# Gate and up products of an expert job in one pass of 256 columns, in a two-layer encoder with a mixture of experts

## What is computed

```
...
def expert_block(args):
    xblk, e = args
    return (jax.nn.silu(xblk @ w1[e]) * (xblk @ w3[e])) @ w2[e]
...
x = x + _hier_moe(_rmsnorm(x, ffn_norm_w[l]), ..., expert_w_gate[l], expert_w_up[l], expert_w_down[l])
...
```

## Time and profile before

| | us |
|---|---|
| median of 3 runs | 1587.78 |
| lowest and highest | 1585.37, 1592.27 |
| the profiled execution | 1591.66 |
| its span, first to last instruction | 1589.8 |
| TensorE busy (matmul records) in the span | 1325.3 (83%) |
| VectorE busy | 661.5 (42%) |
| ScalarE busy | 461.5 (29%) |
| HBM read | 488.09 MB, 308 GB/s over the span |

### The profile page before, as it was taken

One profiled execution on the slowest core, in us unless ns is written; L12 is line 12 of the kernel. 1 busy time (PEld: TensorE's weight loads), 2 busy tenths in 40 slices (PEclk: granted clock), 3 DMA queues, 4 the chain that ended last, 5 costly groups with the idle time before them and its releaser, 6 DMA issues. The chain is left out here.

```text
span 1589.8 us, 46384 instructions
## 1 busy us (share of the span) xinstructions
PE 1325.3 (83%) x19436; PEld 1016.1 (64%) x19437; DVE 661.5 (42%) x1618; ACT 461.5 (29%) x952; POOL 120.8 (8%) x108
## 2 busy tenths in 40 slices
PE   7998899998788776678799988999888887776775
PEld 6787687766555554455578876787666655554554
DVE  6666856663222111112186777666622221111112
ACT  3455645542111100001054565554411110100101
POOL 2002530000000000000020045200000000000000
PEclk9998999999999888989999999999999998888888
DMA  9531224589999999999974220445999999999996
GB/s 342 201 128 54 67 93 173 211 356 380 425 424 428 429 427 427 428 428 427 413 270 159 106 83 30 159 166 209 389 414 410 426 428 427 427 429 427 428 428 267
DMA packets 80204, 490.60 MB, mean 309 GB/s; under 512 B 13263, under 2 KB 15847, under 8 KB 52455
## 3 DMA queue, kind: packets, MB, share of 16 engines
q1 hardware_dynamic: 80102, 489.16, 75.8%
HBM read 488.09 MB, written 1.05 MB: 308 GB/s over the span
## 5 line engine op out<-in xcount | busy, mean ns | idle before, releaser
L2067 PE MATMUL ps<-ring,arena 128*32 128x128 f32 x5504 | 204.0, 308 | 119.1 <-DMA ring<-in_expert_w_gate_dram 75.0
L2067 PEld LDWEIGHTS ps<-ring,arena 128*32 128x32 f32 x5504 | 177.0, 124 | 157.7 <-DMA ring<-in_expert_w_gate_dram 77.2
L2149 ACT ACTIVATE arena<-ps 128x128 f32<-128x128 f32 x66 | 18.3, 278 | 479.8 <-PE ps L2067 479.8
L2067 PE MATMUL ps<-arena 128*32 128x128 f32 x2688 | 98.7, 305 | 51.1 <-DMA arena<-in_expert_w_gate_dram 34.6
L2250 DVE COPY arena<-ps 128x256 f32<-128x256 f32 x68 | 28.9, 425 | 249.2 <-PE ps L2033 249.0
L2067 PEld LDWEIGHTS ps<-arena 128*32 128x32 f32 x2688 | 86.1, 124 | 69.9 <-DMA arena<-in_expert_w_gate_dram 39.9
L489 POOL TENSOR_TENSOR small<-small,cst 128x8 f32<-128x8 f32 (+1 forms) x21 | 27.7, 1318 | 1209.6 <-DVE small L763 450.4
L1822 DVE TENSOR_TENSOR w_low<-ring,w_high 128x512 fp32r<-128x512 f32 x126 | 85.7, 705 | 51.8 <-ACT w_high L1746 51.8
L2091 PE MATMUL ps<-ring,arena 128*32 128x256 f32 x1440 | 94.6, 399 | 9.9 <-DMA ring<-in_expert_w_down_dram 6.8
L2311 DVE TENSOR_TENSOR arena<-ps,arena 128x128 f32<-128x128 f32 x66 | 25.0, 380 | 185.1 <-ACT arena L2149 185.1
L1746 ACT ACTIVATE w_high<-ring 128x512 fp32r<-128x512 f32 x126 | 77.2, 635 | 74.3 <-PE ps L1682 62.0
(11 more groups left out here) (374 smaller groups left out, 2474.7 us busy)
## 6 DMA issues: line engine op xcount, KB each, us to landing
ring<-in_expert_w_gate_dram SPq DMA_DIRECT2D x42, 2048.0 KB, 40.3
ring<-in_expert_w_up_dram SPq DMA_DIRECT2D x42, 2048.0 KB, 40.6
ring<-in_w_in_dram SPq DMA_DIRECT2D x28, 2048.0 KB, 7.7
ring<-in_expert_w_down_dram SPq DMA_DIRECT2D x22, 2048.0 KB, 41.2
ring<-in_expert_w_down_dram SPq DMA_DIRECT2D x44, 1024.0 KB, 37.4
arena<-in_expert_w_up_dram SPq DMA_DIRECT2D x20, 2048.0 KB, 41.0
arena<-in_expert_w_gate_dram SPq DMA_DIRECT2D x20, 2048.0 KB, 39.8
arena<-in_expert_w_down_dram SPq DMA_DIRECT2D x20, 2048.0 KB, 41.7
```

The costliest lines, as they stand in the source:

```text
L2067: ins = pe.matmul(bank_b[32 * g:32 * g + 32, u * P:(u + 1) * P], xg[:, c], spare[u][:, c, g] if from_spare else w[:, u, c, g], start=(c == ...
```

## The change

For the very first job of a layer (i = 0, k = 0) all stays as it was. Every other job waits for its gate slot and its up slot, then runs 32 matmuls of 256 columns, each with the gate columns and the up columns of one (c, g) side by side, into the first 256 columns of `bank_b`; then it counts `m_gu` up. The gather of job J + 1 comes behind this pass. SP waits for `m_gu` ahead of both loads of the pair, except for the first job's gate slot, for which it still waits for `m_gate`. For the job of expert 3 to read both spare slots in one view, `tenth` and `eleventh` become the halves of one tensor, `spare_pair`; their places in memory are the same.

```diff
@@ -135,8 +135,10 @@
     x_sb = sb("x_sb", NT * D_MODEL)
     hT = sb("hT", KC * SEQ)
     assert start_of["hT"] == start_of["x_sb"] + 4 * NT * D_MODEL
-    tenth = nc.alloc_sbuf_tensor_at("tenth_slot", [P, 4096], F32, offset=start_of["x_sb"])
-    eleventh = sb("eleventh_slot", 4096)
+    sb("eleventh_slot", 4096)
+    assert start_of["eleventh_slot"] == start_of["x_sb"] + 4 * 4096
+    spare_pair = nc.alloc_sbuf_tensor_at("spare_pair", [P, 2 * 4096], F32, offset=start_of["x_sb"])
+    tenth, eleventh = spare_pair[:, 0:4096], spare_pair[:, 4096:2 * 4096]
     xn = sb("xn", NT * D_MODEL)
     cst = sb("cst", K_ALL)
     arena = sb("arena", 16160)
@@ -1914,7 +1916,7 @@
                 def refill(i, k, load, pair=True):
                     count(i, k)
                     if pair:
-                        sp.wait_ge(m_gate, sp.snap(ended))
+                        sp.wait_ge(m_gate if isinstance(i, int) and (i, k) == (0, 0) else m_gu, sp.snap(ended))
                         load(i, 3 * k)
                         sp.wait_ge(m_gu, sp.snap(ended))
                         load(i, 3 * k + 1)
@@ -2053,22 +2055,28 @@
                     pe.wait_ge(m_xg, J)
                     landing = i * 16 + 16 if isinstance(i, int) else pe.snap(i * 16 + 16)
                     w = gate_up(k)
-                    spare = [t[:, :].rearrange("p (c g f) -> p c g f", c=KC, g=4) for t in (tenth, eleventh)]
-                    for u in range(2):
-                        from_spare = k == 0 and isinstance(i, int) and i == 1
-                        if from_spare:
-                            pe.wait_ge(m_land[3 * SETS + u], (32, 16)[u])
-                        elif k == 0:
-                            pe.wait_ge(m_land[u], max(i * 16, 16) if isinstance(i, int) else pe.snap(i * 16))
+                    if k == 0 and isinstance(i, int) and i == 0:
+                        for u in range(2):
+                            pe.wait_ge(m_land[u], 16)
+                            for c in range(KC):
+                                for g in range(4):
+                                    ins = pe.matmul(bank_b[32 * g:32 * g + 32, u * P:(u + 1) * P], xg[:, c], w[:, u, c, g],
+                                                    start=(c == 0), stop=(c == KC - 1))
+                            ins.then_inc((m_gate, m_gu)[u], 1)
+                    else:
+                        if k == 0 and isinstance(i, int) and i == 1:
+                            w = spare_pair[:, :].rearrange("p (u c g f) -> p u c g f", u=2, c=KC, g=4)
+                            pe.wait_ge(m_land[3 * SETS], 32)
+                            pe.wait_ge(m_land[3 * SETS + 1], 16)
                         else:
-                            pe.wait_ge(m_land[3 * k + u], landing)
+                            for u in range(2):
+                                pe.wait_ge(m_land[3 * k + u], pe.snap(i * 16) if k == 0 else landing)
                         for c in range(KC):
                             for g in range(4):
-                                ins = pe.matmul(bank_b[32 * g:32 * g + 32, u * P:(u + 1) * P], xg[:, c], spare[u][:, c, g] if from_spare else w[:, u, c, g],
+                                ins = pe.matmul(bank_b[32 * g:32 * g + 32, 0:2 * P].rearrange("p (u f) -> p u f", u=2), xg[:, c], w[:, :, c, g],
                                                 start=(c == 0), stop=(c == KC - 1))
-                        ins.then_inc((m_gate, m_gu)[u], 1)
-                        if u == (1 if isinstance(i, int) and i == 0 and k == 0 else 0):
-                            gather(pe.snap(J + 1))
+                        ins.then_inc(m_gu, 1)
+                    gather(pe.snap(J + 1))
                     pe.wait_ge(m_selwT, J)
                     pe.wait_ge(m_y, J)
                     scatter()
```

## The result

The changed kernel takes 1594.17 us (median of 20 runs) against 1588.16 us for the kernel before, run beside it; the ratio is 1.003, with a 95% interval of 1.0019 to 1.0041, that is 3.0 to 6.5 us more (the two medians by themselves are 6.0 us apart). A change of 0.3% is thus told from none, though the prediction thought only 0.5% could be. Two later comparisons gave 1.0032 (1.0016 to 1.0047) and 1.0034 (1.0018 to 1.0049). The profiled execution of the changed kernel has a span of 1589.3 us, near the 1589.8 us of the one before, so the spans of two single executions do not show the difference; the stages have to be taken apart.

The account below looks back on a forecast made before the run. Weight loading was taken to bound the expert stage, at 428 GB/s. The end of layer 1 (+4.3 us), the end of layer 0 (+2.6) and the start of layer 1 (-1.5) gave +5.4, so 1593.2 us; range 1588 to 1597.5.

Parts of the forecast that it names:

- Price of the pass: TensorE, each job: fused pass 3.50 us, as much as two passes; a job bound by TensorE 8.65 us against 8.53.
- rival 3: Fused pass cheaper than two, 0.6 of them or 2.1 us: +1.6 us, 1589.4; chance 0.03.
- Mid-stage: Middle of the expert stage: loads queued eight deep, so later slot release costs nothing and 428 GB/s stays.
- The ends: Last up slot to down pass: 8.45 us in both layers, +4.3 us in layer 1, +2.6 us in layer 0.
- the clock: Fused pass after rest runs a slow stretch at 1.2 GHz, adding 1.55 us at each end.
- Rival 2: Slow stretches miss the last two jobs: 6.90 us at both ends, +2.3 us, 1590.1; chance 0.16.
- The start of layer 1: First jobs of layer 1's expert stage: fewer issue stalls cut DMA idle from 2.5 to 1.0 us, -1.5 us.
- the upper bound: Start of layer 1: all issue stalls gone, if code comes at a fixed rate; -2.5 us.
- The sum: Whole kernel: 4.3+2.6-1.5 = +5.4 us, 1593.2 us, +0.34%.
- Rival 1: Code as late as now: a 1.4 us stall in a last job, no relief in layer 1; +9.1 us, 1596.9; chance 0.14.

Follow-up runs that it names:

- late_release: Kernel before, with SP giving the gate slot back only after the up pass, for all but the first job; 1591.78 us, ratio 1.0017.
- second profile: The kernel before, unaltered, profiled once more; 1588.99 us.
- padded: Changed kernel, with 32 extra matmuls of 4 columns ahead of the fused pass in the unrolled jobs behind the first; 1599.02 us.
- last_split: Changed kernel, with the very last expert job of each layer back to two passes and the gather between them; 1584.99 us, ratio 0.9977.
- early_fused: Changed kernel, with only the five unrolled jobs fused and loop and last jobs in two passes; 1584.78 us, ratio 0.9977.

## Why the prediction was right

**Price of the pass.** Right: 3.45 us from the pass to the gather, against 3.50, and 3.29 us from gather to down pass, against 3.40; a job bound by TensorE takes 8.49 us against 8.65. The cheaper wide pass of rival 3 (2.1 us) does not show.

**Mid-stage.** Right: 428 GB/s, streams of 417.4 to 418.9 us in layer 0 in every kernel, also in late_release.

**The ends.** Forecast 8.45 us each. Measured 8.68, 8.04 and 8.59 in layer 0, 8.46, 9.65 and 8.27 in layer 1. The terms measured are 1.71 us for the wider pass (3.50 less the 1.88 of the up pass by my rows, 1.62), 0.86 for the gather (3.40-2.31 = 1.09) and 1.3 to 2.9 for the clock (1.55). Rival 2, slow stretches that miss, did not occur in any of six ends. What was mis-sized is the reference of layer 1: 4.19 us is the end without a slow stretch; in the second profile it is 5.86 us, so that the loss there is 8.8-5.0 = 3.8 us by the means of the profiles, not 4.3.

**The start of layer 1.** The sign and the place were right, the size was too small: I took 1.5 us back, with 2.5 as the most; streams say 3.7 us (423.14 to 419.48). What was mis-sized is the stalls. For those ahead of expert 2's gate slot I added up the idle times of the earlier trace rows, 0.91+2.33 = 3.24 us, and took 0.7 of them, 2.3 us. But the two jobs in question took 22.16 us where two without stalls take 2 x 8.53 = 17.06, so the stalls cost 5.1 us. The listed idle time begins only at the end of the last matmul's length, and matmuls follow each other at less than that length; two stalls of 0.17 and 0.18 us were left out besides. And all of them went, as the upper bound had it; padded brought stalls back. So the slot came back not 2.0-2.3 = 0.3 us sooner but 3.5 us (27.2 us after the first load, 30.7 before, 31.8 in the second profile). The seventh load then came before the six ahead of it were through (29.4 us at 4.90 a slot), and the tenth likewise: all of the 2.53 us of idle time that I had counted went, not 1.5. The bytes agree in size. A window of 60 us from the stage's first load, in the kernel before and in the changed one (columns of the earlier trace rows):

```profile
1148.90:1208.90 60.00, 51.94 (x1284) 37.74 (x1280) 14.85 (x47) 6.54 (x18) 0.00 (x0) 0.97 0.98 398
```

```profile
1148.90:1208.90 60.00, 59.66 (x1189) 35.83 (x1181) 18.17 (x60) 9.01 (x23) 0.00 (x0) 1.00 0.99 413
```

15 GB/s over 60 us are 2.1 us of loading; in the second profile of before the rate is 393, 2.8 us. The streams of these two are 4.2 and 3.1 us longer than the changed kernel's mean, so 2.1 and 0.3 us remain. In the first profile the remainder lies near the last landing, where the 16 DMA engines ended unevenly. The microsecond in which the last up slot landed (1572.66) has a DMA share of 0.48 there, and so has the whole microsecond ahead of the landing, while the one ahead of the landing (1567.92) has 1.02 in the changed kernel:

```profile
1572.00:1573.00 1.00, 0.57 (x19) 0.34 (x16) 0.42 (x1) 0.00 (x0) 0.00 (x0) 1.00 0.48 188
```

```profile
1567.00:1568.00 1.00, 0.08 (x4) 0.11 (x8) 0.00 (x0) 0.00 (x0) 0.00 (x0) 1.00 1.02 426
```

That this unevenness comes from the empty queue at the start was not tested, and the second profile does not show it.

**The sum.** +5.4 us forecast; measured +4.8 to +5.4 by the ratios. By the profiles the parts are 2.6 (end 0) + 3.8 (end 1) - 3.7 (start) - 0.4 (stream 0) = +2.3 us. So some 2.5 to 3 us of the measured difference are not in these parts; last_split and early_fused, too, are 1.5 to 3.5 us less fast against the kernel before than their stages promise. Which executions were profiled accounts for about as much. The two of the kernel before (1591.66 and 1588.99 us) lie 3.5 us above and 0.4 below the medians of their batches, the three of the changed kernel (1591.17, 1590.60, 1594.51) 3.0 and 1.6 us below and 0.7 above: on the means 1.5 us too long and 1.3 too short, 2.8 us together, in the direction that is missing. In which stage the executions that were not profiled differ from these is not known. The time outside the streams and ends differed by up to 8 us from one profile to another (733 to 741 us), with no order by kernel that I can see; 4.5 us of it lie ahead of the first expert job, where all kernels run the same instructions.

With the start at -3.7 and the end of layer 1 at +3.8, my own sum would have been +2.7 us and the forecast 1590.5. The agreement of the total with the forecast is thus partly luck, its mechanism is not.

**Rival 1** (code late in the last job) is refuted: no stall for issue in the fused pass of any last job. Its other half, that the stalls stay, as well.

## What to carry to other kernels

In a stage fed by a deep queue of loads, what runs between two landings is free, and a wait that merges two landings moves that work behind the second: price it at the last tile of the stage, not in the middle, and treat that tile by itself. Wide instructions are worth most where the code is new and the queue is empty, at the start of a stage. When the profile shows stalls in a pass, price them by the distance from one job to the next and not by the idle times listed. Here the fused pass in all but the first and the last job beats both kernels, at 0.9977 and 0.9963 of the kernel before, and so does the fused pass in the five unrolled jobs alone, at 0.9977.

## What the runs showed of the hardware

TensorE stood still 0.2 to 3.1 us at a time in unrolled code and the first turns of the loop while DMA was saturated: with some 456 records a job, several stalls at each stage start, with 328 hardly any (one of 0.27 us in the first profile of the changed kernel, one of 0.17 in the second), and with 128 short ones put back they were there again. In layer 1 two jobs of 17.06 us took 22.16 us by them, 5.1 us more, where the view lists 3.6 us of idle time. The last fused pass of a layer, behind 4.3 to 6.0 us of rest, lasted 4.9 to 6.5 us instead of 3.66, with a granted clock of 0.50 in part of it; an extra product of 1.95 us ahead of it, which left 2.9 us of rest, brought it back to 1.00.
